# S5 tables and first-quarter rows of a RetNet/S5 layer formed ahead of and between the k and v evacuations

## The reference, cut to what matters

```
proj = rmsnorm(x) @ w_in                      # -> q | k | v | g | u, 512 columns each
q, k = rope(q), rope(k) * 128**-0.5           # 4 heads of 128
o, s_new = retention(q, k, v, state)          # decay gamma_h = 1 - 2**(-5-h)
y_ret = silu(g) * head_layernorm(o, ret_gn)
# S5: 32 groups of 16 channels, a 64-dim complex diagonal state each
ab = exp(a * dt);  bb = f(a, dt) * b          # discretised A and B
h_t = ab * h_(t-1) + bb u_t                   # complex scan over the tokens
y_s5 = gelu(Re(C h) + d_skip * u);  y_s5 *= sigmoid(y_s5 @ w_glu + b_glu)
x += concat(y_ret, y_s5) @ w_out
```

## Time and profile before

| | us |
|---|---|
| median of 3 runs | 2433.82 (2433.69, 2433.82, 2440.07) |
| the profiled execution, its own time | 2445.67 |
| its span | 2443.9 |
| PE busy | 2303.1 (94%) |
| DVE busy | 1255.6 (51%) |
| POOL busy | 1220.1 (50%) |
| ACT busy | 338.3 (14%) |
| mean granted clock of PE | 0.947 |

### The profile page before, as it was taken

The page is one execution under the profiler, slowest core; times in us unless marked ns, Lnnn a source line. Parts: engine busy times, 40 slices in busy tenths (PEclk is TensorE's granted clock), DMA queues, the critical chain, the costliest instruction groups (busy, mean ns, idle before and its releaser), DMA issues.

```text
span 2443.9 us, 39468 instructions
## 1 busy us (share of the span) xinstructions
PE 2303.1 (94%) x16133; PEld 2129.0 (87%) x16133; DVE 1255.6 (51%) x2169; ACT 338.3 (14%) x579; POOL 1220.1 (50%) x1185
## 2 busy tenths in 40 slices
PE   7978888999999999999999989999989999999997
PEld 7977778979999999999999955587579799999996
DVE  6698886332626245675656434432444327254363
ACT  4211212221100000120120222100211210000001
POOL 5546677624566556766766500022035256655562
PEclk8989998999999999999999977788889899999998
DMA  5212334311222222233343311331131012222221
GB/s 180 87 52 91 114 110 172 115 45 53 86 72 85 86 86 78 90 125 129 144 160 132 107 77 59 141 132 69 56 138 70 35 70 80 77 87 86 86 70 55
DMA packets 37171, 231.28 MB, mean 95 GB/s; under 512 B 4396, under 2 KB 7468, under 8 KB 11696
## 3 DMA queue, kind: packets, MB, share of 16 engines
q1 hardware_dynamic: 21600, 154.15, 17.8%
q10 hardware_dynamic: 15440, 75.21, 7.9%
HBM read 195.50 MB, written 33.85 MB: 94 GB/s over the span
## 4 chain that ended last, share of the span: by engine, by line
PE 77%; DVE 17%; issue 2%; ACT 2%; POOL 1%; DMA 0%; DVEq 0%; ACTq 0%; POOLq 0%
PE psum L502 60%; PE psum L532 15%; PE psum L518 1%; DVE hl L1880 1%; DVE hh L1876 1%; DVE tm L1573 1%; DVE xc L1945 1%; DVE CA L1586 1%; DVE xnl L1405 1%; DVE tm L2159 1%; DVE tm L2158 1%; POOL wlo L454 1%; DVE xnl L2161 1%; DVE hr L1869 0%; DVE hs L1872 0%
## 5 line engine op out<-in xcount | busy, mean ns | idle before, releaser
L452 POOL TENSOR_SCALAR whi<-raw 128x512 fp32r<-128x512 f32 x584 | 422.6, 724 | 1135.0 <-PE psum L502 1101.4
L454 POOL TENSOR_TENSOR wlo<-raw,whi 128x512 fp32r<-128x512 f32 x584 | 801.9, 1373 | 48.7
L502 PE MATMUL psum<-xnh,whi 128*128 128x288 f32 (+1 forms) x2816 | 627.3, 301 | 42.6 <-DVE xnl L1405 17.6
L502 PE MATMUL psum<-xnl,whi 128*128 128x288 f32 (+1 forms) x2816 | 620.8, 299 | 0.0
L502 PE MATMUL psum<-xnh,wlo 128*128 128x288 f32 (+1 forms) x2816 | 619.9, 298 | 0.0
L502 PEld LDWEIGHTS psum<-xnh,whi 128*128 128x128 f32 x2816 | 467.3, 193 | 52.7 <-issue 37.6
L502 PEld LDWEIGHTS psum<-xnl,whi 128*128 128x128 f32 x2816 | 467.2, 193 | 0.0
L502 PEld LDWEIGHTS psum<-xnh,wlo 128*128 128x128 f32 x2816 | 466.6, 192 | 0.0
L502 PE MATMUL psum<-hh,whi 128*128 128x288 f32 x1024 | 218.7, 295 | 2.1 <-DVE hl L1880 2.1
L502 PE MATMUL psum<-hl,whi 128*128 128x288 f32 x1024 | 219.1, 295 | 0.0
L502 PE MATMUL psum<-hh,wlo 128*128 128x288 f32 x1024 | 217.5, 293 | 0.0
(11 more groups left out here) (394 smaller groups left out, 2784.8 us busy)
## 6 DMA issues: line engine op xcount, KB each, us to landing
raw<-in_w SPq DMA_DIRECT2D x146, 1024.0 KB, 4.8
C<-in_C ACTq DMA_DIRECT2D x4, 1024.0 KB, 4.9
o_cp<-mvt ACTq DMA_DIRECT2D x4, 1024.0 KB, 3.9
o_cs<-C ACTq DMA_DIRECT2D x4, 1024.0 KB, 4.0
t_xc<-xc ACTq DMA_DIRECT2D x3, 1152.0 KB, 6.6
t_z<-mv ACTq DMA_DIRECT2D x3, 1152.0 KB, 4.2
t_q<-mq ACTq DMA_DIRECT2D x3, 1152.0 KB, 4.2
t_k<-mk ACTq DMA_DIRECT2D x3, 1152.0 KB, 4.2
```

The costliest lines, as they stand in the source:

```text
L452: pool.tensor_scalar(whi[:, s, c], raw[:, s, c], 1.0, 1.0, ALU.mult, ALU.mult).then_inc(S("slab_hi"), 1)
L454: ins = pool.tensor_tensor(wlo[:, s, c], raw[:, s, c], whi[:, s, c].bitcast(F32), ALU.subtract)
L502: ins = pe.matmul(bank(g, 2 * m + b)[:, 0:t1 - t0], W[wi][:, kk, m0 + m, :], r[:, kk, t0:t1], start=(at_first and wi == 0 and r is rh), st ...
```

## The change

VectorE forms doublings 1 and 2 ahead of the evacuation of k0, doubling 4, `unit_circle` and doubling 8 between k0 and k1, doubling 16 between k1 and v0, and 32, `unit_circle` and 64 between v0 and v1. After v1 come `i32`, the copies of the tables' tail, `input_rows(0)` and `output_rows(0)`, and only then `evac_g(0)` and `evac_g(1)`. `output_rows(0)` no longer stands behind the aux evacuation of head 0. In the last quarter `split_glu(2)` runs ahead of `ret_y(3)`; for this q[3] and k[3] change slots. The instructions themselves, their number and their shapes stay the same, and nothing changes on PE, ScalarE, POOL and SP.

```diff
--- before.py
+++ after.py
@@ -317,8 +317,8 @@
         glus.close()
 
         qk = sb("qk", [P, 2 * RET_H, T], on=l0a)
-        q = [qk[:, c, :] for c in (0, 3, 4, 6)]
-        k = [qk[:, c, :] for c in (1, 2, 5, 7)]
+        q = [qk[:, c, :] for c in (0, 3, 4, 7)]
+        k = [qk[:, c, :] for c in (1, 2, 5, 6)]
         memx1a = qk[:, 0:3, :].rearrange("p a t -> p (a t)")[:, 0:6 * MEM].rearrange("p (k t) -> p k t", k=6)
         kt = sb("kt", [P, NCH, P], on=l0a)
         sq = sb("sq", [P, T], on=l0a)
@@ -1541,21 +1541,29 @@
                 step(lambda: tt(s1, s1, t, ADD))
                 squared()
 
-            evac_rope(1, 0)
-            evac_rope(1, 1)
-            step(lambda: v.tensor_copy(mrs, mrs0))
-            v.sem_inc(S("rope_free"), 1)
-            for i in range(2):
+            def evac_v(i):
                 g = GR["rs", "v", i]
                 group_ready(v, g)
                 for t, (b, c0) in enumerate([(0, 0), (1, 0), (2, 0), (3, 0), (3, 256)]):
                     r = P if t < NTB else TS
                     ins = ts(vt[0:r, t, 256 * i:256 * i + 256], bank(g, b)[0:r, c0:c0 + 256], rsc[0:r, t:t + 1], None, MUL)
                 ch.mark(ins, free[g % 2])
-                for n in ((1, 2, 4, 8), (16, 32))[i]:
-                    doubling(n)
-                    if n in (4, 32):
-                        unit_circle()
+
+            doubling(1)
+            doubling(2)
+            evac_rope(1, 0)
+            doubling(4)
+            unit_circle()
+            doubling(8)
+            evac_rope(1, 1)
+            step(lambda: v.tensor_copy(mrs, mrs0))
+            v.sem_inc(S("rope_free"), 1)
+            doubling(16)
+            evac_v(0)
+            doubling(32)
+            unit_circle()
+            doubling(64)
+            evac_v(1)
             step(lambda: v.tensor_reduce(i32[:], ident[:].rearrange("p (a c) -> p c a", a=4), AX.X, ADD))
 
             def evac_g(i):
@@ -1605,14 +1613,15 @@
                 step(lambda: v.tensor_copy(rt[:], rho))
                 step(lambda: v.memset(rt[:, :, 0:1], 0.0), lambda: v.memset(rt[:, :, N5 + 1:N5 + 2], 0.0))
 
-            evac_g(0)
-            doubling(64)
             one = lambda z: z[:, :, N5:N5 + 1].rearrange("p s o -> p (s o)")
             step(lambda: v.tensor_copy(ctab[:, :, N5 + 1:W5], ctab[:, :, 0:W5 - N5 - 1]),
                  lambda: v.tensor_copy(stab[:, :, N5 + 1:W5], stab[:, :, 0:W5 - N5 - 1]),
                  lambda: v.tensor_copy(one(ctab), R(44)), lambda: v.tensor_copy(one(stab), R(45)))
             input_rows(0)
+            output_rows(0)
+            evac_g(0)
             evac_g(1)
+
             def low_memory(l):
                 for kk in range(DT):
                     v.wait_ge(S("mem_hi"), 8 * l + kk + 1)
@@ -1709,8 +1718,6 @@
                     ts(kt[:, j, :], bank(g, 1)[:, P * j:P * j + P], dec[:, h % 2, at:at + 1], None, MUL)
                 ins = ts(kt[0:TS, NTB, :], bank(g, 2)[0:TS, 0:P], dec[0:TS, h % 2, TS - 1:TS], None, MUL)
                 ch.mark(ins, free[g % 2], S("ret_w"))
-                if h == 0:
-                    output_rows(0)
                 if h == 2:
                     low_memory(1)
                     rotate_back(h)
@@ -1746,11 +1753,10 @@
                     decay_columns(h + 1)
                     output_rows(h + 1)
                 else:
-                    split_glu(0)
-                    split_glu(1)
+                    for j in range(3):
+                        split_glu(j)
                 memory_keys(MEM_SLABS[4 * h + 3])
             ret_y(RET_H - 1)
-            split_glu(2)
             split_glu(3)
             group_ready(v, GR["mem", 1, "v", 3])
             for a in range(2):
```

## The result

| | before | after |
|---|---|---|
| median, 20 runs each | 2437.59 us | 2432.38 us |
| lowest to highest | 2432.13 to 2441.08 | 2420.59 to 2435.97 |
| ratio, with 95% interval | | 0.9974 (0.9965 to 0.9983) |
| the profiled execution's span | 2443.9 | 2429.6 |

A forecast was written before the change was run, and what follows sets the result against it. The prediction took PE's waits on VectorE as the bound. Aux 5.0 us, G's `CA` 3.1 and G's clock 1.4 gave 9.5 us off a median of 2433.8: 2424.3 us, range 2419 to 2432.

The forecast's parts named there:

- Steps 1 to 6: VectorE's new timetable from 91.5 us, from doublings 1 and 2 through v1's evacuation, ending at 149.6 us.
- Step 4: k1's evacuation with POOL idle, 5.3 us, and the memory norm's copy, 0.5: ends at 121.0, no wait counted.
- step 5: Doubling 16, v0, doubling 32 and `unit_circle`: 19.4 us less 2.5 for POOL's pause at doubling 32, to 137.9.
- The added wait: PE ahead of g1 stands for v1's evacuation, from 146.4 to 149.7: 3.3 us.
- Step 7: After v1: `i32` 0.4, tails 0.8, `input_rows` 3.5, `output_rows` 8.3 us, to 162.6; sum of the rows unchanged.
- The sum: Gain through G: aux 5.0 us earlier, `CA` ready 3.1, G at full clock 1.4, slab nothing; together 9.5 us.
- the first term: Aux starts at 172.4 instead of 177.39: 5.0 us gained.
- step 9: From the start of `evac_g(1)` to aux: 8.0 us instead of 7.5, so aux starts at 172.4.
- steps 1 and 3: Doublings 1 and 2, 7.7 us; doubling 4 with `unit_circle` beside a split, 6.6 (factor 2.2); doubling 8, 3.9.
- mostly eaten on VectorE before 150 us: Rival, chance 0.22: doubling 64 and rope evacuations cost more, VectorE 6 us later at aux; total 2430 us.
- the second: Rival, chance 0.20: clock drops ahead of g1 after 3.3 us idle, score 1.2 to 2.9 us later; about 2426.5.
- The split of the third quarter: Near the GLU's start, covered by PE's wait for POOL: gain taken as 0, bounds -0.5 and +0.5 us.

The follow-up runs named there:

- e4: The changed kernel, but POOL waits for `ca_ready` before it splits the first memory slab; ratio to before 0.9977.
- e1: The kernel before with only the q[3] and k[3] slots changed and `split_glu(2)` ahead of `ret_y(3)`; ratio to before 0.9998.
- e8: Changed kernel: v1 behind doubling 32, `evac_g` behind `input_rows`, `low_memory` behind score evacuation, `output_rows` behind aux evacuation, POOL's second-memory-slab split held until `ca_ready`; ratio to before 0.9947.
- e10: e8 without the hold: POOL splits the second memory slab as soon as PE begins the first; ratio to before 0.9967.
- e6: Changed kernel: v1 behind doubling 32, `evac_g` behind `input_rows`, then `output_rows`, `low_memory` and decay columns between score and aux evacuations; ratio to before 0.9967.
- e9: e8 with doubling 1 and the table start moved between q0 and q1; ratio to before 0.9953.
- e2: The changed kernel with `split_glu(2)` back behind `ret_y(3)`, the slots staying changed; ratio to before 0.9978.

## Why the prediction was wrong

**The bound was named rightly.** VectorE's list sets the score, and three waits of PE hang on it. The idle ahead of k0, k1 and v0 went, the new wait ahead of g1 came, G's wait went, and most of the gain was still there at the GLU (4.4 us).

**Steps 1 to 6 were mis-sized by 4.3 us** (v1 free at 78.1 from q, forecast 73.8). Doublings 1 and 2 took 9.2 us (forecast 7.7), doubling 4 with `unit_circle` 8.2 (6.6), k1 with the copy 7.0 (5.8), doublings 16 and 32 with v0 and `unit_circle` 20.7 (16.9); doubling 8 took 2.4 (3.9), doubling 64 8.0 (9.5), k0 4.9 (5.5). The factor for tiny steps beside a split was taken as 2.2 for doubling 4 and `unit_circle`; it was 2.7 (8.2 against 3.0). I had read 1.9 from a pair (121.39 to 129.08) that had more than a fifth of its time to itself, and allowed too little for that. And the prediction's list of splits (92.6, 105.2, 133.9, 146.7) leaves one out that the trace of before shows, from 119.48 to 127.43:

```profile
119.48 0.62 POOL L452 TENSOR_SCALAR whi<-raw 128x512 fp32r<-128x512 f32 x1 [5.81 <-PE psum L518]
...
126.14 1.29 POOL L454 TENSOR_TENSOR wlo<-raw,whi 128x512 fp32r<-128x512 f32 x1
```

In the changed kernel it runs from 119.0 to 127.7. Step 4 counts POOL as idle, but the end of k1 and the copy met this split, and doubling 16 took 6.9 us beside it (122.27 to 129.19) against 5.7 before (138.18 to 143.86). The 2.5 us that step 5 takes off for doubling 32 did not come either: with `unit_circle` it took 11.6 us (131.38 to 142.97) against 11.5 before (143.86 to 155.36), as the split from 133.4 caught it. No run held POOL still beside steps 1 to 6, so that their overrun is contention rests on the traces (a 128 x 16 instruction takes 0.17 to 0.2 us in the pauses and up to 1.3 us beside a split); only for the rows did an experiment, e4, show it.

**The added wait** was 7.44 us and not 3.3, for that reason, beyond the 6 us that the prediction had named as a sign of being wrong. Behind it g1 began at the lower clock and took 14.3 us (153.20 to 167.5) instead of 12.4.

**Step 7 failed in kind.** "I take the rows' sum unchanged": by itself it was 13.0 us against 11.8. But in e4, with no split beside them, the same rows take 7.6 us (154.91 to 162.53), so 5.4 us of the 13.0 are the split's. The timetable had the split start at 150 (74.2 from q); it started at 79.2 from q, when the input rows did, because PE's wait for v1 delays POOL's trigger with it. The delay and the contention were costed as separate items, and they are one: VectorE late makes PE late, PE's late start moves the split onto VectorE's next step.

**The sum.** Aux: forecast 5.0 us earlier, measured 0.1 later. `CA`: 3.1, measured 3.07. G at full clock: 1.4, measured 1.5 (2.9 us from G to K against 4.4). Aux and slab: nothing, measured 0.7 (PE took 8.2 us from aux to G without a wait, against 12.0 with 3.07 of wait). So 5.2 us at K, where 9.5 were forecast, and the first term is more than the whole miss. Its 5.1 us are, to rounding, 4.3 of steps 1 to 6 and 1.2 of step 7, less 0.5 in step 9, which took 7.5 us (169.12 to 176.65) and not 8.0. **The step that failed is thus the timetable of VectorE up to v1**: the price of tiny steps beside a split (steps 1 and 3), a split left out (steps 4 and 5), and a pause of POOL's that was not met (step 5).

**The rivals.** What happened is the first, "mostly eaten on VectorE before 150 us", to which I gave 0.22, though not by the steps that it names: doubling 64 took 8.0 us and k0 4.9. Of the second the clock did drop ahead of g1, but it cost nothing at the score: g1 ended at 92.5 from q and `evac_g(0)` at 93.9. The Trainium skill, in "TensorE: Matmul & The Clock Gate", section "HAM oscillation — how this bites in real kernels", warns of gating by such pauses, and the trace agrees: 0.50 in the window from 152 to 154. I had held the two rivals apart, though the one brings the other. By the Trainium skill's rule in "SBUF — State Buffer", section "SBUF: two separate sides", the shared port pair is locked for a whole instruction. The trace agrees: in the changed kernel the eight instructions of `input_rows` lie beside the eight of POOL's split and take 8.7 us, 1.1 us on average against 0.4 when POOL is still, and POOL's take 1.1 us on average as well. I named the rule and kept out its price, which fits the input rows.

**The split of the third quarter** was right in kind: no part of the gain that can be told (e1), covered by POOL but for 0.6 us of PE's wait.

## What to carry to other kernels

When a step is moved on an engine that another one slows down, as POOL does VectorE here, first draw where the other engine's work will lie after the move, and remember that it may be triggered by the very engine that waits for the step. Tiny dependent instructions cost two to three times their price there. Holding back the other engine by one semaphore, where its result isn't due yet, can be worth more than the order (4.5 us at G against 1.4, in e8 and e10) or nearly nothing (0.2 us in e4), depending on what else is late. When two engines are late together, taking away one wait shows little: look for the second before judging the first.

## What was not expected of the hardware

- Instructions of 128 x 16 elements that take 0.17 to 0.2 us each when POOL is still take up to 1.3 us beside its splits. With `input_rows` eight instructions of each engine take the same time, and POOL barely pays (its split took 8.6 us, against 7.9 in e4, where only the evacuations of g lay beside it), while VectorE pays 5.4 us.
- The clock takes back small gains. For the same matmuls the first memory slab took 8.0 us in e6, behind a stop of 6.20 us, and behind a stop of 2.14 us 6.0 us in e8, 7.3 in e9 and 7.5 in e10 (to the slab's end). Up to there e8 and e10 have the same lists on every engine, so the order of the work alone doesn't decide it; what does is not settled.
- Runs of one kernel spread by up to 18 us (e2), and in the profiled pair 9.1 of 14.3 us of difference arise behind the GLU's start (393.43 against 388.22). Not settled is how much of that is the clock of the stretch from 1500 us on, and what decides it.
